# Expert gates scattered into HBM by accumulating indirect DMAs, and 42 in place of 32 sparse tokens, in a one-core decoder layer

## The chip, the core and the metric

The kernel runs on one NeuronCore of a Trainium2 chip. Its time is the device time of one execution in microseconds, lower is better. The engines are TensorE (PE, with PEld for its weight loads), VectorE (DVE), ScalarE (ACT), GpSimd (POOL) and SyncE (SP). SP and ACT issue direct DMAs; POOL issues the indirect ones, which take row numbers from on-chip memory. All DMAs run on the core's 16 DMA engines. The kernel's matmuls are done in single precision by splitting each operand into a high and a low part.

## The reference, cut to what matters

A decoder layer on 256 tokens of width 2048: a mixer, a cross attention and an expert layer. Only the last changes here. Each token scores 128 keys twice in each of 8 heads, keeps the 16 best of each list, then the 16 best of their 256 sums, and so picks 8 x 16 = 128 of 16384 experts, each with a gate.

```python
s1, i1 = lax.top_k(s[:, :, 0], 16)
s2, i2 = lax.top_k(s[:, :, 1], 16)
cand_s = s1[..., :, None] + s2[..., None, :]
top_s, top_pos = lax.top_k(cand_s, 16)       # per token and head, of 256
gates = softmax(top_s)                        # 8 heads x 16 = 128 a token
u = take(expert_u, experts)                   # rows of 2048
act = gelu(einsum('tkd,td->tk', u, x))
y = einsum('tk,tkd->td', gates * act, take(expert_v, experts))
```

## The kernel before

**Dense and sparse tokens.** The tokens are divided. The first TD = 224 are dense: all 16384 experts are computed for them, and the activations of experts not picked are multiplied by a gate of zero. The last TS = 32 are sparse: for them only the picked rows of the expert tables are fetched.

**Front.** 180 pieces of weights, each 128 x 1024 numbers of 4 bytes (512 KB), carry the mixer, the cross attention and the query projection. Each piece is loaded by SP into one of RAW = 4 buffers, copied to a high part by ACT (`whi`), and its low part (`wlo = raw - whi`) is made by POOL (`rest_of`, L438). PE then multiplies. A piece's buffer is loaded again when its low part is done; `whi` and `wlo` have SPL = 3 buffers, freed by PE.

**U stage.** 256 pieces hold the first expert table. Two pieces are a chunk of 128 experts (128 chunks). `u_piece` does per piece 8 wide matmuls (L1885: high weights, moving 448 columns, the tokens' high and low parts side by side) and 8 narrow ones (L1888: low weights, 224 columns). DVE joins the two halves of the sums (`join`, L1234), ACT applies GELU. PE uses three PSUM banks, so chunk c waits for what was done with chunk c-3. POOL makes all the low parts. Early in the stage PE does two sets of key products and DVE the top-k, written between its joins by hand; the tables are there at chunk C_TABLES = 48.

**Gates.** From chunk 54 on PE builds the gates: for each pair of dense tokens two one-hot matmuls of 256 columns (`gate_products`, L1899), 112 pairs. DVE makes the one-hot operands (L1376, L1382), joins the product (L1405) and multiplies it into the activations W (L1412).

**V stage.** 256 pieces of the second table (`v_piece`, L1982 wide and L1985 narrow), the same widths. ACT makes the high part; the low part is made by POOL for the first 8 pieces, then by DVE (`v_step`, L1437), which also splits the gated activations (L1439).

**Sparse rows.** In the V stage POOL gathers quarter rows by indirect DMAs (L465): partition = quarter x 32 + token, 128 x 512 numbers, 128 gathers for each table, into a ring of 12 buffers. DVE takes one after the other: a multiply with sum for table U (L1445), a multiply-add for V (L1458). The functions `taken_u` and `taken_v` say after which piece DVE takes each, and `issued_u`, `issued_v` in which order POOL asks for them; 128 rows in 105 pieces for U.

**Order.** Each engine's program is written out by hand; an engine executes its instructions in that order and waits on semaphores. A wait on DVE thus holds all low parts behind it, and those hold PE.

## Time and profile before

| what | value |
|---|---|
| median of 3 runs | 1914.01 us (1913.36 to 1915.1) |
| profiled execution, its span | 1912.2 us |
| PE busy | 1896.7 us, 11798 matmuls |
| DVE busy | 1383.4 us, 2585 instructions |
| POOL busy | 1390.8 us, 708 instructions |
| ACT busy | 950.5 us |
| DMA | 448.29 MB, mean 234 GB/s |

### The profile page before, as it was taken

Reading aid. Unit: us, or ns where it says so; the run is one execution under the profiler, and the core shown is the slowest. Engines: PE = TensorE matmul, PEld = TensorE weight load, DVE = VectorE, ACT = ScalarE, POOL = GpSimd, SP = SyncE. Lnnn points to the kernel's source line nnn. Section 1 sums busy time; section 2 is a strip of 40 time slices with the busy share of each in tenths; the row PEclk is TensorE's granted clock in tenths of the full one; section 3 lists DMA queues with packets and bytes.
Section 4 is the critical chain, followed back from the end, with each engine's and each line's share of the span. In section 5 each row is a group of like instructions: output and inputs, shape, how many; then the busy total and the mean of one; then the engine's idle time right before and its main releaser. Section 6 shows DMA issues by size and latency. Waiting matters only on the chain.

```text
span 1912.2 us, 35061 instructions
## 1 busy us (share of the span) xinstructions
PE 1896.7 (99%) x11798; PEld 1758.9 (92%) x11798; DVE 1383.4 (72%) x2585; ACT 950.5 (50%) x1342; POOL 1390.8 (73%) x708
## 2 busy tenths in 40 slices
PE   9999999999999999999999999999999999999997
PEld 7888889888999999999999999999999999999997
DVE  7534684045545777968888888479889889999986
...
DMA  8544546564655666666666566689999988999984
GB/s 307 186 143 153 199 144 224 193 190 155 218 188 177 207 209 208 210 202 196 194 192 196 189 195 195 200 280 351 333 336 334 333 297 298 337 325 334 328 273 145
DMA packets 128380, 448.29 MB, mean 234 GB/s; under 512 B 16528, under 2 KB 19472, under 8 KB 127632
## 3 DMA queue, kind: packets, MB, share of 16 engines
...
HBM read 443.04 MB, written 4.19 MB: 234 GB/s over the span
## 4 chain that ended last, share of the span: by engine, by line
PE 72%; POOL 17%; issue 8%; DMA 1%; DVE 1%; ACT 0%; POOLq 0%; SPq 0%; DVEq 0%; ACTq 0%
PE ps L1885 22%; PE ps L1982 22%; POOL wlo L438 17%; PE ps L1888 12%; PE ps L1985 11%; PE ps L1899 1%; PE ps L1585 1%; PE ps L1587 1%; PE ps L1586 1%; PE ps L1961 1%; DMA raw<-in_w_front 0%; PE ps L1869 0%; DMA big<-in_x_t 0%; PE ps L1963 0%; ACT whi L539 0%
## 5 line engine op out<-in xcount | busy, mean ns | idle before, releaser
L438 POOL TENSOR_TENSOR wlo<-raw,whi 128x1024 fp32r<-128x1024 f32 x436 | 1057.6, 2430 | 207.9 <-ACT whi L539 193.1
L539 ACT ACTIVATE whi<-raw 128x1024 fp32r<-128x1024 f32 x435 | 461.2, 1060 | 633.7 <-PE ps L1888 361.8
L1885 PE MATMUL ps<-x_parts,whi 128*128 128x448 f32 x2048 | 588.9, 369 | 0.0
L1982 PE MATMUL ps<-gate_parts,whi 128*128 128x448 f32 x1992 | 573.6, 369 | 0.0
L734 ACT ACTIVATE whi<-raw 128x1024 fp32r<-128x1024 f32 x256 | 271.7, 1061 | 294.9 <-PE ps L1985 255.8
L1888 PEld LDWEIGHTS ps<-x_parts,wlo 128*128 128x128 f32 x2048 | 384.7, 188 | 31.3
L1985 PEld LDWEIGHTS ps<-gate_parts,wlo 128*128 128x128 f32 x1992 | 374.2, 188 | 30.8
L1888 PE MATMUL ps<-x_parts,wlo 128*128 128x224 f32 x2048 | 386.9, 270 | 0.0
L1985 PE MATMUL ps<-gate_parts,wlo 128*128 128x224 f32 x1992 | 376.0, 270 | 0.0
L1437 DVE TENSOR_TENSOR wlo<-raw,whi 128x1024 fp32r<-128x1024 f32 x248 | 303.9, 1225 | 68.1 <-ACT whi L734 52.1
L1885 PEld LDWEIGHTS ps<-x_parts,whi 128*128 128x128 f32 x2048 | 310.3, 191 | 0.0
L1982 PEld LDWEIGHTS ps<-gate_parts,whi 128*128 128x128 f32 x1992 | 301.2, 191 | 0.1
L1585 PE MATMUL ps<-whi,x_parts 128*128 128x512 f32 (+1 forms) x544 | 214.1, 394 | 2.3 <-DVE wlo L888 2.3
L1587 PE MATMUL ps<-whi,x_parts 128*128 128x512 f32 (+1 forms) x544 | 210.1, 386 | 0.0
L1586 PE MATMUL ps<-wlo,x_parts 128*128 128x512 f32 (+1 forms) x544 | 209.4, 385 | 0.0
L465 POOL DMA_INDIRECT gather_low<-in_w_v,big x88 | 115.9, 1317 | 110.7 <-DVE big L1458 80.3
L465 POOL DMA_INDIRECT gather_low<-in_u_rows,big x88 | 103.9, 1180 | 67.3 <-DVE big L1445 54.3
L1234 DVE TENSOR_REDUCE big<-ps 128x224 f32<-128x448 f32 x128 | 79.4, 620 | 88.2 <-PE ps L1888 87.7
L1585 PEld LDWEIGHTS ps<-whi,x_parts 128*128 128x128 f32 x544 | 102.5, 188 | 23.8 <-DVE x_parts L868 3.5
L1587 PEld LDWEIGHTS ps<-whi,x_parts 128*128 128x128 f32 x544 | 102.6, 189 | 21.7
L1586 PEld LDWEIGHTS ps<-wlo,x_parts 128*128 128x128 f32 x544 | 102.7, 189 | 20.2
L1439 DVE TENSOR_TENSOR gate_parts<-big,gate_parts 128x224 fp32r<-128x224 f32 x256 | 112.7, 441 | 1.1 <-ACT gate_parts L737 0.6
...
## 6 DMA issues: line engine op xcount, KB each, us to landing
raw<-in_w_u SPq DMA_DIRECT2D x256, 512.0 KB
raw<-in_w_v SPq DMA_DIRECT2D x256, 512.0 KB
raw<-in_w_front SPq DMA_DIRECT2D x180, 512.0 KB
...
```

The source lines that it names most:

```text
L438: nc.gpsimd.tensor_tensor(wlo[:, j % SPL, :], raw[:, j % RAW, :], whi[:, j % SPL, :], ALU.subtract).then_inc(lo_done, 1)
L465: nc.gpsimd.indirect_dma_start(ROW[at_row], None, table, bass.IndirectOffsetOnAxis(index.bitcast(I32), 0)).then_inc(row_in[at_row], 16)
L539: nc.scalar.activation(whi[:, j % SPL, :], raw[:, j % RAW, :], ACT.Copy).then_inc(hi_done, 1)
L734: nc.scalar.activation(whi[:, (V0 + j) % SPL, :], raw[:, j % RAW, :], ACT.Copy).then_inc(hi_done, 1)
L1437: nc.vector.tensor_tensor(wlo[:, s, :], raw[:, j % RAW, :], whi[:, s, :], ALU.subtract).then_inc(lo_v_done, 1)
L1585: nc.tensor.matmul(out_ap, sh, mh, start=start, stop=False)
L1586: nc.tensor.matmul(out_ap, sh, ml, start=False, stop=False)
L1587: return nc.tensor.matmul(out_ap, sl, mh, start=False, stop=stop)
L1885: nc.tensor.matmul(sums[:, 0:2 * TD], whi[:, s, cols], x_parts[:, :, m, 0:TD], start=m == 0, stop=False, skip_group_check=True)
L1888: ins = nc.tensor.matmul(sums[:, TD:2 * TD], wlo[:, s, cols], xh[:, m, 0:TD], start=False, stop=m == DC - 1, skip_group_check=True)
L1982: nc.tensor.matmul(sums[:, 0:2 * TD], whi[:, s, cols], gate_parts[:, g, :, 0:TD], start=False, stop=False, skip_group_check=True)
L1985: ins = nc.tensor.matmul(sums[:, TD:2 * TD], wlo[:, s, cols], gate_parts[:, g, 0, 0:TD], start=False, stop=False, skip_group_check=True)
```

## The change

- The dense tokens become 214 and the sparse ones 42. PE's moving widths become 428 and 214. P // 3 = 42 tokens are three times on the partitions (GROUPS = 3, 126 rows), and each group handles 43 of a token's 128 experts (PER = 43). A gather now brings 128 whole rows of 2048 numbers (1.049 MB); there are 43 for each table, 86 in all, into a ring of 3. `taken` spreads them over pieces 18 to 121 and 128 to 234 of the V stage.
- The gate products on PE, their one-hot operands and joins on DVE are gone. A scratch tensor in HBM of 16384 experts x 224 numbers (14.7 MB) is filled with zeros in the front by 16 DMAs on ACT's queue. After the top-k, DVE computes the cell of each gate, and POOL adds the gates into the scratch by 256 indirect DMAs of single numbers, one for each of 128 slots and two blocks of tokens (128 and 96 partitions). Before the DMAs of a head it waits for those of the head before in the same block.
- Then POOL loads the gates back, 4 chunks at a time (32 loads, two buffers), and DVE multiplies them into W (`scale_by_gate`): 24 between the joins of chunks 112 to 126, 8 in the first pieces of the V stage.
- POOL's low parts in the U stage end with piece 71, and DVE takes one of twelve before that (`low_u`, piece 10 of a body). From piece 72 on DVE makes all low parts of the U stage, and all of the V stage.
- The top-k is written more densely (`topk_work`: a join after every 4200 ns of work as estimated in the code) and ends within 36 chunks. One of its lists of values now lies in PSUM, so that the sums of candidates have one operand in SBUF.
- At the end the three partial sums of the sparse tokens are moved to the same partitions by DMAs and added by DVE.

```diff
-C_TABLES, C_GATE = 48, 54
-C_ONES = C_GATE - 2
-TD, TS, PARTS, PD = 224, 32, 4, 512
-TOK_PAIRS = TD // 2
-RING = 12
+C_TABLES = 36
+E_BODIES = C_TABLES // CHUNKS_PER_BODY
+GROUPS = 3
+TS = P // GROUPS
+TD = T - TS
+PER = -(-P // GROUPS)
+PITCH = -(-TD // 16) * 16
+PER_LOAD = 4
+LOADS = NK // PER_LOAD
+SCALED_FROM, SCALED_IN_U = 112, 24
+RING = 3
...
-def issued_v(e):
-    return 117 + e if e < RING else taken_v(e - RING) + 1
-
-
-def taken_v(e):
-    return 132 + e * 21 // 25
...
+ROWS_FROM, WEIGHTS_AT_PIECE, ROWS_UNTIL = 18, 127, 234
+ADDED_AT = (*range(240, 239 + GROUPS), 251)
+
+
+def taken(n):
+    if n < PER:
+        return ROWS_FROM + n * (WEIGHTS_AT_PIECE - 6 - ROWS_FROM) // PER
+    return WEIGHTS_AT_PIECE + 1 + (n - PER) * (ROWS_UNTIL - WEIGHTS_AT_PIECE) // PER
...
+TOPK_NS = 4200
...
+        def low_of_u(i, j, late):
+
+            if late:
+                return lo_u_done, i * BODY + (j + 1 - E_BODIES * (BODY - 1))
+            if j == U_VECTOR:
+                return lo_u_done, i + 1
+            return lo_done, i * (BODY - 1) + (U0 + j + (j < U_VECTOR))
+
+        def low_of_v(i, j):
+
+            return lo_v_done, i * BODY + (j + 1)
...
+            with pool.Fori(U0 // BODY, U0 // BODY + E_BODIES) as i:
+                for j in range(BODY):
+                    if j != U_VECTOR:
+                        rest_of(i * BODY, j)
+
+            pool.wait_ge(zeros_out, 16 * NK // (2 * PER_LOAD))
+            pool.wait_ge(cells_ready, 1)
+            for head in range(PH):
+                for tb in range(TB):
+                    if head:
+                        pool.wait_ge(scattered[tb], 16 * TOPK * head)
+                    tokens = min(P, PITCH - tb * P)
+                    for k in range(TOPK * head, TOPK * (head + 1)):
+                        nc.gpsimd.indirect_dma_start(gates_d, bass.IndirectOffsetOnAxis(CELLS[0:tokens, tb, k:k + 1].bitcast(I32), 0),
+                                                     TOP_GATES[0:tokens, tb, k:k + 1], None,
+                                                     compute_op=ALU.add).then_inc(scattered[tb], 16)
+            for tb in range(TB):
+                pool.wait_ge(scattered[tb], 16 * TOPK * PH)
+
+            def load_gates(k):
+
+                if k >= 2:
+                    pool.wait_ge(scaled_by_gate, k - 1)
+                pool.dma_start(gates_of[:, k % 2].rearrange("p a b -> p (a b)"),
+                               gate_rows[:, k * PER_LOAD * PITCH:(k + 1) * PER_LOAD * PITCH]
+                               ).then_inc(gates_in[k % 2], 16)
+
+            def gather(n):
+
+                if n < RING:
+                    pool.wait_ge(used, V0)
                 else:
-                    pool.wait_ge(used, V0 + 4 + d)
-                gather(d % RING, u_rows, IDX[0][:, d:d + 1])
-
-            def gather_v(e):
-
-                if e < RING:
-                    pool.wait_ge(rows_taken, P - RING + (e + RING - P % RING) % RING + 1)
-                else:
-                    pool.wait_ge(rows_taken, P + e - RING + 1)
-                gather(e % RING, v_rows, IDX[1][:, e:e + 1])
-
-            asked = [0, 0]
-            for j in range(OPENING, 2 * NK):
-                if j == OPENING:
-                    pool.wait_ge(picks, 1)
-                    pool.wait_ge(used, V0)
-                while asked[0] < P and j >= issued_u(asked[0]):
-                    gather_u(asked[0])
-                    asked[0] += 1
-                while asked[1] < P and j >= issued_v(asked[1]):
-                    gather_v(asked[1])
-                    asked[1] += 1
-            assert asked == [P, P]
...
+            for k in range(SCALED_IN_U + 2):
+                load_gates(k)
+            pool.wait_ge(picks, 1)
+            for n in range(RING):
+                gather(n)
+            for k in range(SCALED_IN_U + 2, LOADS):
+                load_gates(k)
+            for n in range(RING, 2 * PER):
+                gather(n)
...
+            def zero_gates(q):
+                act.wait_ge(zeros_ready, 1)
+                some = 2 * PER_LOAD * PITCH
+                act.dma_start(gate_rows[:, q * some:(q + 1) * some],
+                              gates_of.rearrange("p a b c -> p (a b c)")).then_inc(zeros_out, 16)
...
+            def low_u(n0, n):
+                dve.wait_ge(hi_done, n0 + (U0 + n + 1))
+                nc.vector.tensor_tensor(wlo[:, (U0 + n) % SPL, :], raw[:, n % RAW, :], whi[:, (U0 + n) % SPL, :],
+                                        ALU.subtract).then_inc(lo_u_done, 1)
+
             def join(k0, c):
 
                 dve.wait_ge(used, k0 * 2 + (U0 + 2 * (c + 1)))
                 sums = ps[:, c % ACT_BANKS, 0:2 * TD].rearrange("p (h t) -> p t h", h=2)
-                late = not isinstance(k0, int) or k0 + c >= C_ONES
-                nc.vector.reduce_sum(LATE[:, c % ACT_BANKS, :] if late else W[:, k0 + c, :], sums, AX).then_inc(sums_joined, 1)
+                nc.vector.reduce_sum(W[:, k0 + c, :], sums, AX).then_inc(sums_joined, 1)
+                if not isinstance(k0, int) or C_TABLES - 2 <= k0 + c < NK - 2:
+                    low_u(k0 * 2, 2 * c + 4)
...
-            v = small(ROWS, 2, TOPK)
+            v = (small(ROWS, TOPK), ps[:, 3, 0:ROWS * TOPK].rearrange("p (r k) -> p r k", r=ROWS))
...
+            cells = CELLS.rearrange("p a b -> p (a b)")
+            step(nc.vector.scalar_tensor_tensor(cells, CH[:, 0, :], float(NK), CH[:, 1, :], ALU.mult, ALU.add))
+            dve.wait_ge(token_in, 16)
+            for tb in range(TB):
+                ins = nc.vector.tensor_scalar(CELLS[:, tb, :].bitcast(I32), CELLS[:, tb, :], float(PITCH),
+                                              stats[:, TOKEN + tb:TOKEN + tb + 1], ALU.mult, ALU.add)
+            ins.then_inc(cells_ready, 1)
...
+            def scale_by_gate(k):
+                dve.wait_ge(act_taken, PER_LOAD * (k + 1))
+                dve.wait_ge(gates_in[k % 2], 16 * (k // 2 + 1))
+                some = W[:, PER_LOAD * k:PER_LOAD * (k + 1), :]
+                nc.vector.tensor_tensor(some, some, gates_of[:, k % 2, :, 0:TD], ALU.mult).then_inc(scaled_by_gate, 1)
+
+            scaled = 0
+            for c in range(SCALED_FROM // CHUNKS_PER_BODY * CHUNKS_PER_BODY, NK - 1):
+                join(0, c)
+                while scaled < SCALED_IN_U * (c + 1 - SCALED_FROM) / (NK - 1 - SCALED_FROM):
+                    scale_by_gate(scaled)
+                    scaled += 1
+            assert scaled == SCALED_IN_U
...
-            def gate_products(i, j):
-
-                pe.wait_ge(hot1, i * PAIRS_PER_BODY + (j + 1))
-                pe.wait_ge(hot2, i * PAIRS_PER_BODY + (j + 1))
-                if not (isinstance(i, int) and i == 0 and j < 2):
-                    pe.wait_ge(gated, i * PAIRS_PER_BODY + (j - 1))
-                for m in range(2):
-                    ins = nc.tensor.matmul(ps[:, 4 + j % 2, m * 2 * P:(m + 1) * 2 * P], hot1_row[:, m, :],
-                                           hot2_rows[:, j % 2, m].rearrange("p a b -> p (a b)"), start=True, stop=True)
-                ins.then_inc(gate_mat, 1)
...
-            def u_row(slot):
-                dve.wait_ge(row_in[slot % RING], 16 * (slot // RING + 1))
...
+            def row_taken(n):
+                dve.wait_ge(row_in[n % RING], 16 * (n // RING + 1))
+                row, k = ROW[n % RING], n % PER
+                weight = WEIGHTS[:, k:k + 1]
+                if n < PER:
+                    ins = nc.vector.tensor_tensor_reduce(row, row, X_GAINED, 1.0, 0.0, ALU.mult, ALU.add, SUMS[:, k:k + 1])
+                elif k == 0:
+                    ins = nc.vector.tensor_scalar(X_GAINED, row, weight, None, ALU.mult)
+                else:
+                    dve.wait_ge(rows_taken, n)
+                    ins = nc.vector.scalar_tensor_tensor(X_GAINED, row, weight, X_GAINED, ALU.mult, ALU.add)
+                ins.then_inc(rows_taken, 1)
...
-                while done[0] < P and j >= taken_u(done[0]):
-                    u_row(done[0])
-                    done[0] += 1
...
+                while done < 2 * PER and j >= taken(done):
+                    row_taken(done)
+                    done += 1
```

POOL's program, at the end of its low parts, of the kernel before (gather_low and x_back hold the ring):

```order
L438 TENSOR_TENSOR wlo<-raw,whi 128x1024
L458 REGISTER_ALU
L458 COMPARE_AND_BRANCH
L465 DMA gather_low<-in_u_rows,big 128x512 x8
L465 DMA x_back<-in_u_rows,big 128x512 x4
```

and of the changed kernel at the same place:

```order
L475 TENSOR_TENSOR wlo<-raw,whi 128x1024
L499 REGISTER_ALU
L499 COMPARE_AND_BRANCH
L512 DMA gates_scratch<-big 3670016x1 x256
L522 DMA gates_of<-gates_scratch 128x896 x26
L532 DMA x_back<-in_u_rows,big 128x2048
L532 DMA gather_low<-in_u_rows,big 128x2048 x2
L522 DMA gates_of<-gates_scratch 128x896 x6
```

The 256 additions and 26 loads of gates now stand between the last low part and the first gather.

DVE's program in the V stage, while rows of table U are taken, of the kernel before (ISA is the multiply with sum and the reading of its sum):

```order
L1437 TENSOR_TENSOR wlo<-raw,whi 128x1024
L1439 TENSOR_TENSOR gate_parts<-big,gate_parts 128x224
L1445 ISA x_back,big<-x_back,big 128x512
L1445 ISA big 128x1
L1445 ISA gather_low,big<-gather_low,big 128x512
L1445 ISA big 128x1
L1437 TENSOR_TENSOR wlo<-raw,whi 128x1024
```

and of the changed kernel:

```order
L1458 TENSOR_TENSOR wlo<-raw,whi 128x1024
L1460 TENSOR_TENSOR gate_parts<-big,gate_parts 128x214
L1458 TENSOR_TENSOR wlo<-raw,whi 128x1024
L1460 TENSOR_TENSOR gate_parts<-big,gate_parts 128x214
L1468 ISA gather_low,big<-gather_low,big 128x2048
L1468 ISA big 128x1
L1458 TENSOR_TENSOR wlo<-raw,whi 128x1024
```

One or two quarter rows a piece became one whole row in two or three pieces.

DVE's program late in the U stage of the changed kernel (`gates_of` holds the loaded gates):

```order
L1303 TENSOR_REDUCE big<-ps 128x214
L1296 TENSOR_TENSOR wlo<-raw,whi 128x1024 x2
L1445 TENSOR_TENSOR big<-big,gates_of 128x856 x2
L1303 TENSOR_REDUCE big<-ps 128x214
L1296 TENSOR_TENSOR wlo<-raw,whi 128x1024 x2
L1445 TENSOR_TENSOR big<-big,gates_of 128x856
```

The multiplications by gates stand in DVE's queue behind a join and ahead of the next two low parts.

## Rows read from the trace of the kernel before

**Rows 1.** the page: busy time and parts 2 and 3, forty slices of 47.8 us

```profile
PE 1896.7 (99%) x11798; PEld 1758.9 (92%) x11798; DVE 1383.4 (72%) x2585; ACT 950.5 (50%) x1342; POOL 1390.8 (73%) x708
DMA  8544546564655666666666566689999988999984
```

**Rows 2.** the chain of waits, share of the span by engine

```profile
PE 72%; POOL 17%; issue 8%; DMA 1%; DVE 1%; ACT 0%; POOLq 0%; SPq 0%; DVEq 0%; ACTq 0%
```

**Rows 3.** waits of PE: who it waited for, us in total, times, longest

```profile
PE ps L1585 <- DVE wlo L888: 2.3, 1, 2.3
```

**Rows 4.** windows: us, busy us (x instructions) by engine, clock, DMA share, GB/s

```profile
660.00:720.00 60.00, 60.00 (x383) 57.07 (x382) 43.95 (x161) 28.33 (x37) 57.51 (x25) 1.00 0.66 209
1279.50:1289.50 10.00, 10.00 (x65) 9.53 (x64) 8.14 (x14) 5.52 (x9) 5.12 (x4) 1.00 1.02 396
1290.00:1300.00 10.00, 10.00 (x65) 9.53 (x64) 9.68 (x21) 5.28 (x9) 8.17 (x7) 1.00 0.99 358
1380.00:1440.00 60.00, 60.00 (x383) 57.07 (x382) 53.60 (x106) 32.15 (x48) 34.39 (x30) 1.00 0.95 337
```

**Rows 5.** line L1885: duration ns min/median/max, first and last start us

```profile
L1885 PE MATMUL ps<-x_parts,whi x2048: 362/367/452, 571.3 to 1250.8; 128*128 128x448 f32 x187
```

**Rows 6.** timeline of PE in the U stage: start us, us, what, count

```profile
700.46 0.38 PE L1888 MATMUL ps<-x_parts,wlo 128*128 128x224 f32 x2
700.67 0.57 PE L1885 MATMUL ps<-x_parts,whi 128*128 128x448 f32 x2
```

**Rows 7.** timeline of PEld there: two narrow loads, then two wide

```profile
700.26 0.39 PEld L1888 LDWEIGHTS ps<-x_parts,wlo 128*128 128x128 f32 x2
700.57 0.30 PEld L1885 LDWEIGHTS ps<-x_parts,whi 128*128 128x128 f32 x2
```

**Rows 8.** the gate matmuls L1899, and one pair of them in the timeline

```profile
L1899 PE MATMUL ps<-hot_rows,hot_row x224: 280/282/285, 854.7 to 1215.9; 128*128 128x256 f32 x112
903.53 0.40 PE L1899 MATMUL ps<-hot_rows,hot_row 128*128 128x256 f32 x2
903.77 0.56 PE L1885 MATMUL ps<-x_parts,whi 128*128 128x448 f32 x2
```

**Rows 9.** timeline of DVE in the V stage

```profile
1400.85 0.68 DVE L1445 CUSTOM_DVE_ANT_0 x_back<-x_back,big 128x512 f32<-128x512 f32 x1
1401.46 1.22 DVE L1437 TENSOR_TENSOR wlo<-raw,whi 128x1024 fp32r<-128x1024 f32 x1
1402.60 0.38 DVE L1439 TENSOR_TENSOR gate_parts<-big,gate_parts 128x224 fp32r<-128x224 f32 x1
1402.90 0.69 DVE L1445 CUSTOM_DVE_ANT_0 x_back<-x_back,big 128x512 f32<-128x512 f32 x1
1403.84 1.23 DVE L1437 TENSOR_TENSOR wlo<-raw,whi 128x1024 fp32r<-128x1024 f32 x1 [0.24 <-issue]
```

**Rows 10.** lines by form on DVE: busy us, mean ns of one

```profile
L1289 DVE TENSOR_TENSOR big<-big 128x256 f32<-128x256 f32 x16 | 26.5, 1696 | 0.0
L868 DVE SCALAR_TENSOR_TENSOR x_parts<-ps,big,x_parts 128x256 fp32r<-128x256 f32 x32 | 13.5, 478 | 31.6 <-ACT x_parts L560 31.6
```

**Rows 11.** timeline of POOL: gathers issued back to back

```profile
1271.42 0.96 POOL L465 DMA_INDIRECT gather_low<-in_u_rows,big  x1 [0.30 <-issue]
1272.69 0.95 POOL L465 DMA_INDIRECT gather_low<-in_u_rows,big  x1 [0.30 <-issue]
...
1401.20 1.15 POOL L465 DMA_INDIRECT gather_low<-in_u_rows,big  x1 [1.57 <-DVE big L1445]
1402.66 1.15 POOL L465 DMA_INDIRECT x_back<-in_u_rows,big  x1 [0.31 <-issue]
1404.11 1.77 POOL L465 DMA_INDIRECT x_back<-in_u_rows,big  x1 [0.30 <-issue]
1406.24 0.94 POOL L465 DMA_INDIRECT x_back<-in_u_rows,big  x1 [0.36 <-DVE big L1445]
```

**Rows 12.** DMA issues: KB each, us from issue to landing

```profile
big<-x_scratch ACTq DMA_DIRECT2D x4, 64.0 KB, 2.5
```

579 lines of the change are left out of this document (246 added, 333 removed).

## The prediction

> **What bounds the kernel now.** I read the page first. PE is busy 1896.7 of 1912.2 us [rows 1], and the chain of waits gives it 72% of the span [rows 2]. The 17% of POOL there say little: the waits of PE name one wait of 2.3 us at the start as the longest, and the others are smaller [rows 3]. So PE is fed on time, and what counts is the pace at which it starts matmuls. The windows give it: 383 matmuls in 60 us in the U stage and in the V stage alike, 16 a piece, which is 60/383 x 16 = 2.507 us a piece, at the full clock of 1.00, the level of 2.4 GHz [rows 4]. 512 pieces are 1284 us, two thirds of the span. The reader is to see also how near the others are. The DMA's line stands at 9 in most slices of the V stage [rows 1], its share is 0.95 at 337 GB/s there, against 0.66 at 209 in the U stage [rows 4], and DVE is busy 53.6 of 60 us. A change that takes work from PE in the V stage must find room there.
>
> **Gate products, removed.** A pair of gate matmuls stands between a narrow and a wide one: it starts at 903.53, and the next wide one at 903.77, so it costs 0.24 us [rows 8]. There are 112: 26.9 us of PE's own time, gone. DVE's work for them (one-hots, joins, products) goes too; PE never waited for it, so I cost that at nothing. What replaces it in the U stage is on DVE two low parts a chunk of 1.14 us (1401.46 to 1402.60) [rows 9] beside a join: under 3 us of the 4.9 of a chunk. ACT's work is no more than before.
>
> **Narrower matmuls.** Two narrow matmuls take 0.21 us from start to start (700.46 to 700.67) [rows 6], 0.105 each, and the four of a group 0.627, so a wide one 0.208. A column at 2.4 GHz is 0.417 ns. 448 to 428 columns gives 8.3 ns, 8 times a piece: 67 ns. For the narrow ones the bounds are 0 and 10 x 0.417 x 8 = 33 ns. Their 224 columns last 93 ns, less than the 105 of their step. The load records tell why: of two loads in 0.39 us with 0.19 each, the second begins at 700.46, the next load at 700.57 [rows 7], and its matmul at 700.67 [rows 6]. A load follows a load after 0.11 us and its matmul 0.10 later, so the load sets the step and fewer columns give nothing. I take 0: 67 ns a piece, 2.440 us, 34.3 us over 512. The Trainium skill (TensorE: Matmul & The Clock Gate, LDWEIGHTS) says that a load's time goes with its columns, 128 at 1.2 a ns, which is 107 ns. By that rule the sum is the same, and the trace agrees with 0.11 us; a rule of columns alone would make it 51.2.
>
> PE alone would then need 1912.2 - 26.9 - 34.3 = 1851.0 us.
>
> **Zeros and memset.** 16 stores of 0.92 MB go out among the front's loads. DMA stands at 4 to 6 tenths there after the first slice [rows 1] and four loads are in flight, which hides them; uncovered, 14.7 MB at 337 GB/s would be 44 us, but no slice of the front is full enough for more than a few us. I take 0, with 5 as upper end. The memset on POOL lies ahead of its first low part, which waits anyway.
>
> **Denser top-k.** DVE must keep PE's pace of 4.88 us a chunk with a join in each 4.2 us of work. The sum of candidates costs 1696 ns for 256 elements with both operands in SBUF while POOL works, where an instruction of 256 elements with one operand in PSUM takes 478 [rows 10]. 16 of them save 19 us. Work of 4.2 us, a join of 428 sums (0.30 for 224 elements, 1402.60 to 1402.90, and 1.05 ns for each more [rows 9], 0.51) and a sixth of a low part are 4.90, as much as PE takes. I take 0, upper end 10 us, since a low part of DVE is due one chunk after its join.
>
> **The additions, from POOL's last low part to the first use of a gate.** The U stage goes from 571.3 to 1250.8 [rows 5]. Of 679.9 us, 641.8 are its pieces and 26.9 the gates, which leaves 11 for the key products. In the changed kernel piece 71 starts at 571.3 + 11 + 71 x 2.44 = 755.5, and POOL is free some 2.4 us before: 753. DVE needs gate 0 when chunk 112 is joined: 571.3 + 11 + 226 x 2.44 = 1134. In these 381 us POOL issues 256 DMAs, the last must land and the first load too, twice 2.5 us by a small transfer [rows 12]. So an issue may take 376/256 = 1.47 us. The trace has no addition in HBM, only gathers of 128 rows. Back to back they start every 1.27 us (1271.42 to 1272.69) when DVE has little to do, and in the full V stage after 1.46, 1.45 and 2.13 us (1401.20 to 1406.24) [rows 11], 1.68 in the mean. The longest, of 1.77 us, began at 1404.11, within DVE's low part of 1403.84 [rows 9], which reads two operands from SBUF; POOL seems to wait for its end. In the V stage DVE does such work for 2.05 of 2.51 us, 82%, in the additions' stretch for 2.28 of 4.88, 47%. Between 1.27 and 1.68 that is 1.27 + 0.41 x 0.47/0.82 = 1.50. 256 x 0.03 = 8 us late, less a slack of some 2 on DVE: I take 6. Bounds: 0 (1.27) and 54 (1.68). Behind the waiting multiplication stand the joins and low parts, so PE stops for the whole of it. That an addition on 16 engines may itself be slower than the issue is left to the rival.
>
> **The V stage.** DVE: low part 1.14, gate part 0.30 [rows 9], 1.44 a piece. A row of 512 takes 0.61 (1400.85 to 1401.46), and 1024 elements 1.14 and 224 elements 0.30, so 2048 0.30 + 1824 x 1.05 ns = 2.2. One in 103/43 = 2.40 pieces: 0.92. Sum 2.36 of 2.44 us: DVE fits, with 3% left, where before 1.44 + 1.22 x 0.61 = 2.18 of 2.51 left 13%. DMA: 43 gathers of 1.049 MB in 103 pieces and 43 in 107, with 210 loads of 0.524 MB, are 90.2 + 110.1 = 200.3 MB in 210 x 2.44 = 512.4 us, or 391 GB/s. Before, the rate was 337. What the engines can do: when the ring filled the windows show 396 GB/s at a share of 1.02, then 358 at 0.99 [rows 4], 377 in the mean; 200.3/0.377 = 531.3, 19 us more than PE needs. Bounds: 396, 506 us, nothing lost; and 337/0.95 = 355, 564 us, 52 lost. I take 19: the mean of two windows at the limit. Of the DMA the Trainium skill (DMA: Bandwidth & Descriptors, Where 436 GB/s comes from) says that for HBM to SBUF the 358 of HBM bind. By that figure the 200.3 MB take 559.5 us and the loss is 47. The trace differs in a window of 10 us, where 396 came through, and comes to it in the next.
>
> **The end.** Adding three groups over whole rows puts some 9 us of DVE work into pieces 240 to 252, with about 1 us spare a piece and its tail's product of whole rows beside the last matmuls; stores are 4% smaller. I take 0, bounds -1 and 4.
>
> **Sum.** 1851.0 + 6 + 19 = 1876.0 for the profiled execution. The median of the runs lies 1.8 above its span, so 1878.
>
> **Rivals.** (A) Both covers hold: the additions are issued in under 1.47 us and the DMA carries 391 GB/s. For it: 396 in one window, and rows of 8 KB come in fewer descriptors than those of 2 KB. Against: the mean over any longer stretch. 1853. (B) The V stage is held by DMA and DVE together: with 3% left DVE can't catch up after a late row, and a late row holds the low parts. For it: the share of 0.95 now. Price: the 52 us of the bound in place of 19, and up to 5 more: 1911 to 1916, about the time of before. (C) Slower: the additions are issued, or carried out, too slowly. Place: the first multiplication by gates, at chunk 112. Each 0.1 us of the 256 costs 25.6 us. The gain left is 1914 - 1878 = 36, plus the 6 already counted, so from 1.47 + (42 + 4)/256 = 1.65 us it is slower. For it: 1.68 is the mean of the three issues quoted, 2.13 the longest, and an addition must read, add and write in HBM beside full loads. Against: DVE occupies its operand path half as much there, and half the DMAs have only 96 partitions. At 1.75 us: 72 late in place of 6, 1944. (D) The change doesn't lower the pace at all, widths of 214 starting at odd places: 34 lost, 1912.
>
> **How the numbers follow.** Forecast (one or both covers partly gone, 1858 to 1898): 0.50. A: 0.19. B: 0.12. C: 0.14. D: 0.05. The predicted time is the forecast's, 1878; its own range is 1858 to 1898. The range for 8 in 10 takes A and B in and ends inside C: 1848 to 1922. A measurement tells 0.2%, some 4 us, from no change. Faster by more: the forecast, A, half of B and a fifth of D, in all 0.76, and 0.02 of C: 0.78. Within: 0.06. Slower: 0.16.
>
> **What would show it.** Right: no L1899 rows; 60 us of U stage hold 393 to 394 matmuls (16 x 60/2.44); narrow matmuls still 0.21 us for two. In the V stage the DMA share is at 1.0, the rate above 365 GB/s, and PE waits for DVE low parts that waited for rows or for ACT's high parts behind a load. The additions take 1.4 to 1.6 us from start to start and DVE waits a few us for `gates_of` once. Wrong: narrow steps of 0.20 would give up to 17 us more; a wait of tens of us before L1445 is C; a V stage of 2.44 us a piece is A.

## The result, and the profile after

| | median of the runs | span of the profiled execution | clock of TensorE |
|---|---|---|---|
| before | 1914.55 us (1913.36 to 1915.56, 4 runs) | 1912.2 us | 0.997 |
| after | 2108.41 us (2108.12 to 2112.88, 4 runs) | 2106.9 us | 0.950 |

The changed kernel is slower: the ratio is 1.102, with a 95% interval of 1.100 to 1.103. The forecast was 1878 us in a range of 1848 to 1922.

The page after, its lines of busy time, clock and transfers and its chain of waits; they answer to [rows 1, 2]. A slice is 52.7 us.

```profile
PE 1864.5 (88%) x11578; PEld 1746.1 (83%) x11578; DVE 1362.0 (65%) x1914; ACT 947.8 (45%) x1342; POOL 1256.6 (60%) x629
...
PEclk9999999999999999999999555898999999999999
DMA  8656666658556577777776222799999998999985
GB/s 299 206 174 203 208 245 215 224 178 245 190 183 216 190 212 213 215 212 215 213 215 183 0 0 0 252 308 308 373 367 356 372 371 304 361 363 357 346 302 162
...
POOL 46%; issue 15%; DVE 15%; DMA 13%; PE 9%; ACT 2%; POOLq 0%; SPq 0%; DVEq 0%; ACTq 0%
```

PE is busy 1864.5 us (1896.7 before), 88% of the span in place of 99%. Three slices in the middle move 0 GB/s, and TensorE's clock there is at 0.5, the level of 1.2 GHz. The chain belongs to POOL now, where PE had 72%. The waits after (who waited, for whom, us in total, times, longest), which answer to [rows 3]:

```profile
DVE big L1445 <- DMA gates_of<-gates_scratch: 197.4, 16, 180.6
PEld ps L1903 <- DVE wlo L1296: 187.0, 6, 179.6
PE ps L1903 <- DVE wlo L1296: 186.6, 6, 179.4
ACT whi L787 <- DMA raw<-in_w_v: 183.2, 94, 7.5
POOL wlo L475 <- ACT whi L588: 170.3, 141, 23.9
ACT whi L787 <- PE ps L1972: 146.5, 126, 3.4
```

One wait of 179.4 us is nearly the whole difference of 194.7. L1445 is the multiplication by gates, L1296 a low part queued behind it on DVE. The windows (columns as in [rows 4]) show the U stage early, beside additions, in the stop and after it, and last the V stage:

```profile
660.00:720.00 60.00, 60.00 (x393) 58.53 (x392) 55.07 (x196) 27.37 (x34) 53.21 (x22) 1.00 0.64 211
1060.00:1120.00 60.00, 60.00 (x394) 58.59 (x393) 37.42 (x38) 29.43 (x37) 51.65 (x25) 1.00 0.79 213
1160.00:1220.00 60.00, 0.00 (x0) 0.00 (x0) 0.00 (x0) 0.00 (x0) 49.69 (x34) 0.50 0.21 0
1340.00:1400.00 60.00, 57.04 (x365) 54.76 (x364) 49.09 (x51) 27.75 (x34) 9.49 (x18) 1.00 0.93 330
1460.00:1720.00 260.00, 250.91 (x1600) 241.08 (x1600) 235.17 (x282) 130.84 (x198) 67.74 (x41) 1.00 0.94 363
```

393 and 394 matmuls in 60 us where before had 383: the pace forecast is there. (A window also counts the matmuls under way at its ends. From start to start an undisturbed piece takes 2.454 us, and before 2.520; the forecast had 2.440 and 2.507 from the counts. The difference, on which its sum rests, is the same.) In the third row nothing works but POOL. In the last, 1600 matmuls in 260 us are 2.60 us a piece, slower than before's 2.51 by the same count.

What POOL does then, first beside DVE's low parts with DVE's own timeline, then in the stop (start us, us, what, idle before):

```profile
899.22 2.15 POOL L512 DMA_INDIRECT gates_scratch<-big  x1 [0.31 <-issue]
901.67 2.15 POOL L512 DMA_INDIRECT gates_scratch<-big  x1 [0.30 <-issue]
904.12 2.21 POOL L512 DMA_INDIRECT gates_scratch<-big  x1 [0.30 <-issue]
...
898.84 1.23 DVE L1296 TENSOR_TENSOR wlo<-raw,whi 128x1024 fp32r<-128x1024 f32 x1 [0.37 <-ACT whi L588]
901.29 1.23 DVE L1296 TENSOR_TENSOR wlo<-raw,whi 128x1024 fp32r<-128x1024 f32 x1 [1.23 <-ACT whi L588]
903.81 1.23 DVE L1296 TENSOR_TENSOR wlo<-raw,whi 128x1024 fp32r<-128x1024 f32 x1 [0.43 <-ACT whi L588]
...
1250.04 1.43 POOL L512 DMA_INDIRECT gates_scratch<-big  x1 [0.30 <-issue]
1251.77 1.43 POOL L512 DMA_INDIRECT gates_scratch<-big  x1 [0.30 <-issue]
```

An addition starts 2.45 us behind the one before it, one for each low part of DVE, and 1.73 us with DVE idle. The forecast had 1.50. The additions' line in full (duration in ns, least, median, most; first and last start), and where the U stage began and ended, which answers to [rows 5]:

```profile
L512 POOL DMA_INDIRECT gates_scratch<-big x256: 1427/2087/2547, 759.3 to 1321.2; - x128
L1903 PE MATMUL ps<-x_parts,whi x2048: 352/370/726, 572.7 to 1402.4; 128*128 128x428 f32 x187
L1951 PE MATMUL ps<-gate_parts,whi x48: 367/373/697, 1407.9 to 2092.4; 128*128 128x428 f32 x48
```

They begin at 759, where 753 was forecast, and end at 1321, 187 us after the forecast had gate 0 due (1134). The U stage takes 829.7 us (before 679.5), the V stage 684.8 over all of its matmuls (before 647.6).

### The profile page after: what moved, and what is told of

Its sections match the earlier page's. It is cut to its first block, busy times and chain, and to the rows that moved or that the text cites. A ratio compares the mean times of both kernels' runs of the same rounds, so it can differ in the third digit from the quotient of the medians.

```text
span 2106.9 us, 32603 instructions
## 1 busy us (share of the span) xinstructions
PE 1864.5 (88%) x11578; PEld 1746.1 (83%) x11578; DVE 1362.0 (65%) x1914; ACT 947.8 (45%) x1342; POOL 1256.6 (60%) x629
## 4 chain that ended last, share of the span: by engine, by line
POOL 46%; issue 15%; DVE 15%; DMA 13%; PE 9%; ACT 2%; POOLq 0%; SPq 0%; DVEq 0%; ACTq 0%
POOL wlo L475 23%; POOL gates_scratch L512 23%; DMA raw<-in_w_v 11%; DVE wlo L1458 6%; PE ps L1969 4%; DVE big L1473 2%; PE ps L1972 2%; DVE gather_low L1468 2%; DMA gates_of<-gates_scratch 2%; ACT whi L787 2%; DVE gate_parts L1460 1%; DVE x_back L1468 1%; PE ps L1603 1%; PE ps L1605 1%; PE ps L1604 1%
## 5 line engine op out<-in xcount | busy, mean ns | idle before, releaser
L1903 PE MATMUL ps<-x_parts,whi 128*128 128x428 f32 x2048 | 582.6, 366 | 186.7 <-DVE wlo L1296 186.6
L475 POOL TENSOR_TENSOR wlo<-raw,whi 128x1024 fp32r<-128x1024 f32 x238 | 580.8, 2448 | 173.4 <-ACT whi L588 170.3
L1969 PE MATMUL ps<-gate_parts,whi 128*128 128x428 f32 x2000 | 572.9, 367 | 33.0 <-DVE gate_parts L1460 32.2
L512 POOL DMA_INDIRECT gates_scratch<-big x256 | 480.7, 1878 | 82.8 <-issue 82.8
L1906 PE MATMUL ps<-x_parts,wlo 128*128 128x214 f32 x2048 | 382.7, 268 | 0.0
L1972 PE MATMUL ps<-gate_parts,wlo 128*128 128x214 f32 x2000 | 375.4, 269 | 0.0
L1458 DVE TENSOR_TENSOR wlo<-raw,whi 128x1024 fp32r<-128x1024 f32 x256 | 313.0, 1223 | 80.6 <-ACT whi L787 80.3
L1296 DVE TENSOR_TENSOR wlo<-raw,whi 128x1024 fp32r<-128x1024 f32 x190 | 231.9, 1226 | 131.5 <-ACT whi L588 131.5
L1445 DVE TENSOR_TENSOR big<-big,gates_of 128x856 f32<-128x856 f32 x32 | 33.5, 1048 | 197.6 <-DMA gates_of<-gates_scratch 197.4
L532 POOL DMA_INDIRECT gather_low<-in_v_rows,big x29 | 61.7, 2128 | 148.6 <-DVE big L1473 108.0
L746 ACT ACTIVATE big<-big (+1 forms) x128 | 46.9, 367 | 198.5 <-DVE big L1303 198.5
```

The lines of the kernel that those rows point to most:

```text
L475: nc.gpsimd.tensor_tensor(wlo[:, j % SPL, :], raw[:, j % RAW, :], whi[:, j % SPL, :], ALU.subtract).then_inc(lo_done, 1)
L512: nc.gpsimd.indirect_dma_start(gates_d, bass.IndirectOffsetOnAxis(CELLS[0:tokens, tb, k:k + 1].bitcast(I32), 0), TOP_GATES[0:tokens, tb, k ...
L1296: nc.vector.tensor_tensor(wlo[:, (U0 + n) % SPL, :], raw[:, n % RAW, :], whi[:, (U0 + n) % SPL, :], ALU.subtract).then_inc(lo_u_done, 1)
L1458: nc.vector.tensor_tensor(wlo[:, s, :], raw[:, j % RAW, :], whi[:, s, :], ALU.subtract).then_inc(lo_v_done, 1)
L1903: nc.tensor.matmul(sums[:, 0:2 * TD], whi[:, s, cols], x_parts[:, :, m, 0:TD], start=m == 0, stop=False, skip_group_check=True)
L1906: ins = nc.tensor.matmul(sums[:, TD:2 * TD], wlo[:, s, cols], xh[:, m, 0:TD], start=False, stop=m == DC - 1, skip_group_check=True)
```

## The experiments

There are fourteen, all edits of the changed kernel; where one builds on another the text says so. Stage lengths are from the first to the last start of their matmuls. Those for which no range is given were run once, and differences under 5 us between them are not used.

**Half of the additions.**

```diff
-            for head in range(PH):
+            for head in range(PH // 2):
```

> Leaves out the gates of heads 4 to 7: 128 additions in place of 256, all else as in the changed kernel. Theory 1 (issue-bound additions): the 2.2 us a DMA on POOL is the whole cause of the 180 us stop before chunk 112; 128 x 2.44 = 312 us end at about 1072, ahead of chunk 112 at about 1134, so the stop is gone and the time is 2108 - 180 - 4 (clock at the lower level after the stop) = 1924, still slower than 1914 because the V stage keeps its loss of about 54 us. Theory 2 (the stop comes from the DMA engines, or the read-back of gates is slow by itself): a stop of tens of us stays, 1950 or more.

1924.8 us. The 128 additions stand 2.43 us apart and end at 1068, before they are due, and the stop is gone: the U stage takes 650.7 us. The V stage keeps its length, 680.7. The additions are the stop, and 10 us over the kernel before remain with them out of the way. This kernel is the base of most that follow.

**Writes in place of additions**, all 256.

```diff
-                                                     TOP_GATES[0:tokens, tb, k:k + 1], None,
-                                                     compute_op=ALU.add).then_inc(scattered[tb], 16)
+                                                     TOP_GATES[0:tokens, tb, k:k + 1], None).then_inc(scattered[tb], 16)
```

> The 256 indirect DMAs write the gates in place of adding them (where two heads of a token pick one expert, one gate is lost). Theory 1a (the addition makes the issue dear): the issue falls from 1.43 and 1.54 us to the 0.95 of a gather, spacing 1.25 with DVE idle, about 2.44 with DVE's low parts where it locks to them or less; time 2108 - 60 to 100. Theory 1b (it is the element-wise destination, not the addition): issue unchanged within 0.05 us, time within 5 us of 2108.

1935.9 us. The same numbers to the same cells, written, cost POOL 0.955 us each in place of 2.09:

```profile
L512 POOL DMA_INDIRECT gates_scratch<-big x256: 904/955/2013, 761.4 to 1099.5; - x128
```

They end at 1100 and there is no stop. A write costs what a gather cost ([rows 11], 0.95). So the price that I had carried over from a gather holds for a write, and not for an addition. The time is 70 us and more below what was expected, since the writes do not go at 2.44 us, one for each low part, but at 1.33 in the mean. The trace shows why:

```profile
903.39 0.95 POOL L512 DMA_INDIRECT gates_scratch<-big  x1 [0.30 <-issue]
...
908.44 1.94 POOL L512 DMA_INDIRECT gates_scratch<-big  x1 [0.30 <-issue]
...
903.41 1.23 DVE L1295 TENSOR_TENSOR wlo<-raw,whi 128x1024 fp32r<-128x1024 f32 x1 [1.23 <-ACT whi L587]
...
908.32 1.23 DVE L1295 TENSOR_TENSOR wlo<-raw,whi 128x1024 fp32r<-128x1024 f32 x1 [1.15 <-ACT whi L587]
```

The first write began just ahead of a low part (903.39, 903.41) and was not held, though the low part ran beside all of it. The second began 0.12 us inside one and ended 0.83 us behind its end. Of the 256 writes 21 were held in this way.

**Low parts with one operand in PSUM**, from piece 78 on; they subtract what lies there, and not the high part.

```diff
-                nc.vector.tensor_tensor(wlo[:, (U0 + n) % SPL, :], raw[:, n % RAW, :], whi[:, (U0 + n) % SPL, :],
+                other = ps[:, 4:6, :].rearrange("p a b -> p (a b)") if not isinstance(n0, int) or n0 + n >= C_TABLES * 2 + 6 else whi[:, (U0 + n) % SPL, :]
+                nc.vector.tensor_tensor(wlo[:, (U0 + n) % SPL, :], raw[:, n % RAW, :], other,
```

> DVE's low parts from piece 72 on of the U stage subtract two PSUM banks in place of the high part, so they read one operand from SBUF (their result is meaningless, their length and waits are the same). Theory 1 (POOL's issue waits for the end of DVE instructions with two SBUF operands): the spacing falls from 2.44 to the 1.73 and 1.85 us seen with DVE idle, the 256 end 256 x 0.65 x (161/256 of them were issued beside DVE) earlier, some 105 to 110 us; time about 2000. Rival (POOL is slowed by DMA traffic or by memory, not by DVE): spacing stays above 2.3 us and the time at 2108.

2016.4 us: 92 of the 194 us are back, where about 108 were expected. DVE's instruction takes 1.22 us as before, but POOL no longer waits for its end:

```profile
900.09 1.54 POOL L512 DMA_INDIRECT gates_scratch<-big  x1 [0.31 <-issue]
901.94 1.54 POOL L512 DMA_INDIRECT gates_scratch<-big  x1 [0.30 <-issue]
...
899.93 1.22 DVE L1297 TENSOR_TENSOR wlo<-raw,ps 128x1024 fp32r<-128x1024 f32 x1 [0.37 <-ACT whi L588]
902.38 1.22 DVE L1297 TENSOR_TENSOR wlo<-raw,ps 128x1024 fp32r<-128x1024 f32 x1 [1.23 <-ACT whi L588]
```

1.85 us apart beside DVE, as with DVE idle (1.84 in the mean over all 256). The stop is 86 us. The two causes are apart now: the addition itself (1.85 against 1.27 of a write) and DVE's instructions of two SBUF operands (2.45 against 1.85). They do not test the second. The writes above were held only where they began inside a low part and not where one began behind them, so what waits may be the reading at the start of an issue and not the descriptors.

**32 sparse tokens in place of 42.**

```diff
-GROUPS = 3
+GROUPS = 4
```

> Only the number of groups is set from 3 to 4: 32 sparse tokens, 224 dense, 64 whole rows in place of 86. Theory: the stop stays (POOL's issues are the same; PE reaches chunk 112 some 15 us later, so it is about 165 us) and the V stage loses no more than a few us, since its bytes fall from 391 to about 320 GB/s at PE's pace and DVE's rows from 0.92 to 0.67 us a piece. PE: 2.507 in place of 2.440 us a piece is +34. Sum 2108 - 15 + 34 - 54 = 2073. Rival (the V stage's loss has another cause than rows, as the loads of gates or the restart after the stop): 2120 to 2130.

2106.1 us (2104.1 to 2108.7, 3 rounds), ratio to before 1.100 (1.098 to 1.102), against 1.102 of the changed kernel. The stop is 177. The U stage is slower by PE's pace, 846.2, and the V stage faster, 667.4. Pieces 18 to 234 take 2.54 us each, 4 us over PE's own pace of 2.520 in all, where the changed kernel loses 38. So whole rows cost little as long as fewer of them come: the trace shows 331 GB/s from 1460 to 1720 in place of 363. What stays is the start of the V stage (13 us over PE's pace) and its last 22 pieces (5), and the stop is 12 us longer than the 165 reckoned; the time is 33 us above the 2073 expected. The ten tokens more bring PE what was forecast, and the transfers take it back.

**The first three gathers spread**, with half of the additions.

```diff
             for n in range(RING):
+                load_gates(SCALED_IN_U + 2 + 2 * n)
+                load_gates(SCALED_IN_U + 3 + 2 * n)
                 gather(n)
-            for k in range(SCALED_IN_U + 2, LOADS):
-                load_gates(k)
```

> Gates of heads 4 to 7 are left out, as in the run with half of the additions (1924.8 us, V stage 680.7), so that the stop in the U stage is absent. Here the first three gathers are issued between the last six loads of gates, about at pieces 6, 10 and 14 of the V stage, in place of all at once at its start. Theory: the slow start of the V stage (eight pieces at up to 4.5 us where 2.6 would do, with ACT waiting 6.8 and 7.0 us for a raw piece, and the clock that falls to 0.5 behind it) comes from the 3.1 MB of these gathers in front of the raw pieces; then the first eight pieces take at most 3 us each, the V stage 10 to 15 us less, the time is 1910 to 1915. Rival: the start is slow for the loads of gates and the multiplications that wait for them; then nothing moves by more than 3 us: 1922 to 1928.

1928.2 us, V stage 684.3: no gain, my theory falls. The first eight pieces take 3.6 us each (4.3 in the run with half of the additions), where at most 3 were expected, and pieces 18 to 234 take 7 us more in all. ACT still waits 7.4 us for a raw piece.

**Gathers of half width**, with half of the additions.

```diff
-                nc.gpsimd.indirect_dma_start(ROW[n % RING], None, u_rows if n < PER else v_rows,
+                w = D if n < RING else D // 2
+                table = u_rows if n < PER else v_rows
+                table = table if n < RING else table.rearrange("a (h b) -> (a h) b", h=2)
+                nc.gpsimd.indirect_dma_start(ROW[n % RING][:, (n // RING % 2) * (D - w):(n // RING % 2) * (D - w) + w], None, table,
```

> Gates of heads 4 to 7 are left out, and all gathers but the first three bring half of a row (0.52 MB in place of 1.05), while DVE works on the whole width as before; the sparse tokens' result is not computed. Compare with the run with half of the additions (1924.8 us, V stage 680.7, pieces 30 to 234 at about 2.62 us, where PE alone would need 2.44). Theory, the DMA engines bound the V stage (demand 391 GB/s): the pace goes to 2.45 us, the V stage loses 30 to 35 us, the time is about 1891. Rival, DVE bounds it (2.36 us of work a piece as forecast, more with its waits): the pace stays at 2.6, the time within 5 us of 1925. Half and half: 1905 to 1912.

1908.8 us, V stage 658.5, 22 us shorter: the case between the two rivals. Pieces 18 to 234 take 2.51 us each, where 2.45 was expected if transfers alone held them.

**Row work of half width on DVE**, its counterpart:

```diff
-                    ins = nc.vector.tensor_tensor_reduce(row, row, X_GAINED, 1.0, 0.0, ALU.mult, ALU.add, SUMS[:, k:k + 1])
+                    ins = nc.vector.tensor_tensor_reduce(row[:, 0:D // 2], row[:, 0:D // 2], X_GAINED[:, 0:D // 2], 1.0, 0.0, ALU.mult, ALU.add, SUMS[:, k:k + 1])
...
-                    ins = nc.vector.scalar_tensor_tensor(X_GAINED, row, weight, X_GAINED, ALU.mult, ALU.add)
+                    ins = nc.vector.scalar_tensor_tensor(X_GAINED[:, 0:D // 2], row[:, 0:D // 2], weight, X_GAINED[:, 0:D // 2], ALU.mult, ALU.add)
```

> Gates of heads 4 to 7 are left out, and DVE multiplies or adds only the first 1024 of a row's 2048 numbers; the gathers bring whole rows; the sparse tokens' result is not computed. The counterpart of the run with gathers of half width. Theory, DMA bounds the V stage: the pace stays near 2.6 us, time 1918 to 1927. Rival, DVE bounds it: DVE has 0.36 us less a piece (86 x 1.06 us / 256), the pace goes to 2.45, time about 1891.

1928.1 us, V stage 681.2: nothing. Pieces 18 to 234 take 565 us with half of the additions, 543 with narrow gathers and 567 with short row work. The window from 1300 to 1420 of the run with narrow gathers, and behind it that of the run with short row work:

```profile
1300.00:1420.00 120.00, 119.85 (x777) 116.52 (x776) 114.80 (x139) 64.63 (x97) 32.82 (x21) 1.00 0.86 300
```

```profile
1300.00:1420.00 120.00, 112.72 (x717) 108.11 (x716) 85.74 (x126) 58.23 (x89) 28.00 (x18) 1.00 0.94 358
```

With half the bytes DVE is busy 114.8 of 120 us, 96%, and PE hardly waits. With half of DVE's row work DVE is at 71%, and PE is still idle for 7 us of the 120 and has 717 matmuls, fewer than the other's 777. Of the two it is the transfers that hold the V stage there, and not DVE's row work.

**Writes, 32 tokens and spread gathers**, to see what the design could reach.

```diff
-GROUPS = 3
+GROUPS = 4
```

To this line come the edits of the writes and of the spread gathers, as shown above.

> Writes in place of additions (cells that two heads share keep one gate only), 32 sparse tokens (GROUPS = 4), and the first four gathers but one spread over pieces 6 to 14. It asks what the design could reach if the additions were cheap. From the parts: U stage 645 to 660 us at 2.51 us a piece plus the gap of 4.6 us at 722, V stage 667 less 6 to 12 for the spread gathers, 572.7 before them and 15 behind and between: 1900 to 1915 us, thus at most 0.7% faster than the kernel before, or the same. Rival: the width of 42 tokens is what pays, and this ends slower than the run with writes alone (1935.9).

2247.1 us, 1.173 times before. It missed by over 330 us, and in no part that I had thought of. From 785 to 1122 us PE does hardly anything:

```profile
850.00:950.00 100.00, 15.48 (x35) 10.36 (x36) 3.98 (x4) 3.73 (x5) 75.89 (x80) 0.50 0.05 11
```

The waits of PE over the whole run, most of them in that stretch, are put down to the instruction's issue and not to another engine:

```profile
PE ps L1905 <- issue: 139.9, 64, 3.2
PE ps L1902 <- issue: 138.1, 65, 3.9
```

**The same without the spread** (writes and 32 tokens alone):

> Writes in place of additions and 32 sparse tokens, the gathers at their old place: the run with writes, 32 tokens and spread gathers (2247 us) without its third edit. There PE stood at 70 instructions in 100 us from 785 to 1122 us, at half the clock, while POOL made its 256 writes; with writes and 42 tokens it did not. Theory: the spread has nothing to do with it, writes with 32 tokens do, by how PE's instructions are fetched beside them: again 2240 us. Rival: it hangs on the exact program, and this one runs free: 1920 to 1930.

1923.9 us. The same window:

```profile
850.00:950.00 100.00, 100.00 (x637) 95.17 (x637) 61.05 (x60) 47.85 (x60) 75.85 (x80) 1.00 0.69 207
```

The two programs differ only in POOL's list behind the writes and 26 loads of gates, at the start of the V stage (1242 us in this run). PE did 71 instructions in the 100 us while POOL did 80. Three runs of the stalled program took 2243 to 2248 us, the fourth 6166. It hangs on the exact program, and its cause stays open. It is not that more code was fetched: the page of either run has 40 packets of instructions, 0.66 MB, on queue q8. The run without it answers the question asked: with cheap issues (writes, which lose a gate where two heads pick one expert) the design ends 10 us behind the kernel before (1913.6 on that chip).

**Gains loaded early, gates multiplied from chunk 96**, on top of the spread gathers.

```diff
-SCALED_FROM, SCALED_IN_U = 112, 24
+SCALED_FROM, SCALED_IN_U = 96, 24
...
+            pool.wait_ge(picks, 1)
+            pool.dma_start(X_GAINED, gain_rows[0].partition_broadcast(P)).then_inc(gain_s_in, 16)
```

> Gates of heads 4 to 7 are left out. The first three gathers are spread as in the run before (1928.2 us, V stage 684.3); besides, the 1.05 MB row of gains is loaded in the U stage by POOL's queue in place of at piece 6 of the V stage, and the multiplications by gates begin at chunk 96 in place of 112. Theory: the DMA engines are full (share 1.01) from 1240 to 1255 in that run because rows of x, gains, gates, gathers and raw pieces fall together, and DVE waits 3.5 us for a load of gates at the turn of the stages. Then the gap at the turn (5.2 us) goes, the first eight pieces take under 3.2 us each (4.1 before), the time is 1912 to 1918. Rival: what slows the first pieces is the low clock that follows any gap; without the gap it gains the same in those pieces. Second rival: neither, it is the rows of x (three loads of 336 KB), which stay: 1922 to 1928.

1924.7 us, where the theory had 1912 to 1918. The gap at the turn of the stages is gone and the first eight pieces take 3.1 us each, as the theory had it. But the earlier multiplication met loads of gates that stood behind the gains, and PE waited 7.7 us before 1085; less this wait of my own making the time would be 1917. The second rival, the rows of x, is not out: the time lies in its range, and ACT still waits 6.5 us for a raw piece, at 1239.

**One load of x rows in place of three**, gains early, chunk 112 again.

```diff
-                    for g in range(GROUPS):
+                    for g in range(1):
```

> Gates of heads 4 to 7 are left out, and the rows of x are loaded for the first of three groups only (the others stay unfilled). First gathers spread, gains loaded in the U stage, the gate multiplications from chunk 112 as in the changed kernel. In the run with the latter two edits the packets of the three loads of x rows took 521 to 825 ns beside 310 of a gathered row of the same 8 KB, the DMA engines stood at 0.99 with 216 GB/s, and ACT waited 6.5 us for a raw piece. Theory: these loads make that wait; then it is under 2 us, no gap of PE over 1 us after the turn of the stages, the time 1914 to 1919. Rival: it comes from the gate loads and the sum of all: the wait stays over 4 us, the time 1920 to 1926.

1920.9 us, 2 above the range of the theory and inside that of its rival (1920 to 1926). The wait itself went as the theory had it: ACT's longest for a raw piece near the start is 2.3 us (from 6.5), the first eight pieces take 2.7 us each, and the V stage is 670.5, 8 us shorter than in the run before and 14 shorter than with the spread alone. So the loads of x rows make most of the slow start that was left once gains and gathers were out of their way.

Why they weigh so much is not shown. In the changed kernel they came in from 1416 to 1429, at a full share and a low rate:

```profile
1416.00:1430.00 14.00, 10.02 (x59) 9.30 (x57) 4.00 (x5) 1.78 (x4) 0.57 (x1) 0.85 1.02 258
```

Their 126 packets of 8 KB took 509 ns in the median. But gathered packets of 8 KB took 521 in the same stretch (309 from 1405 to 1700 over all), and the 4 KB packets of raw pieces 250 (159). All transfers were slow together. The Trainium skill (SBUF — State Buffer, Door 1: The DMA port swizzle) has a transfer's rate go by how many of 16 ports its partitions reach. That would be a reason for loads of 42 partitions to crowd the others, and no run here separates it from there being too many transfers at once; with four loads of 32 partitions (the run with 32 tokens) the packets of x rows took 521 ns too.

**The same, and gathers of half width:**

> The run with one load of x rows, and gathers of half width besides. Gates of heads 4 to 7 and the sparse tokens' result are left out. Theory, the V stage has lost its 56 us over PE's pace to two things, transfers at its start and the gathers' bytes: then it takes 635 to 645 us (256 pieces at 2.44 are 624.6) and the time is 1888 to 1898. Rival: a third cost is left, DVE's queue, of 15 us or more: V stage over 650, time over 1902.

1896.3 us, V stage 648.5: the time as expected, the stage 4 us over its range. Of the 57 us that the changed kernel's V stage has over PE's pace, 36 are gone with these edits.

**Additions of 16 gates each**, half of the additions.

```diff
-                    tokens = min(P, PITCH - tb * P)
+                    tokens = 16
```

> The 128 additions of heads 0 to 3 bring 16 gates each in place of 128 or 96 (gates of the other tokens and heads are left out). Compare with the run with half of the additions: 1.54 us for one of 128 with DVE idle, 1.43 for one of 96, 2.15 beside DVE's low parts, one in each of them. Theory: POOL needs 1.1 us whatever the number and 3.6 ns for each (from the 0.12 us between 128 and 96), and locks stand in between: an addition of 16 takes 1.1 to 1.2 us alone and the spacing beside DVE is 1.6 to 2.4. Rival: the time is the length of DVE's instruction, and the spacing stays 2.43. The whole time moves little, 1920 to 1928, since no addition is waited for here.

The rival holds: the durations stay at 2148 ns in the median and the spacing at 2.43, whatever the number.

```profile
L512 POOL DMA_INDIRECT gates_scratch<-big x128: 1274/2148/2280, 760.0 to 1069.1; - x128
```

Two of the 128 began outside a low part; they show the number, 1274 ns where 128 gates take 1534. The theory had 1.6 to 2.4 for the spacing. Smaller additions would not have helped.

The traces tell when the two engines go in step. An issue that begins inside a low part goes on when the low part ends. In the median an addition of 96 or 128 gates then ends 1.31 us behind it, one of 16 gates 1.15 and a write 0.83. With the 0.30 us between two issues the next one begins 1.6, 1.45 or 1.13 us behind the low part. The next low part begins 1.22 us behind it (2.45 less 1.23). Additions of any size here come too late and are held again; writes mostly come before it and are not.

**The first head written**, all gates there, the rest of the additions kept, gathers spread, gains early.

```diff
-                                                     compute_op=ALU.add).then_inc(scattered[tb], 16)
+                                                     compute_op=ALU.add if head else ALU.bypass).then_inc(scattered[tb], 16)
```

> All gates are there. The cells of the first head hold zeros before, so its 32 issues are writes; the other 224 stay additions. The first gathers are spread and the gains are loaded in the U stage. Theory, POOL's issues set the stop, at the prices measured (writes 1.33 us apart, additions 2.44 beside DVE, 1.8 with DVE idle): the writes end near 802, 143 additions fit until 1152, the 81 left take 146 us, and the stop falls from 180 to about 155; the start of the V stage gives 4 to 10 more: about 2076 us, 2070 to 2086. Rival: the stop is set by what comes behind the additions (the first loads of gates, the multiplications, the low clock), and it falls less than 10 us: 2092 to 2104.

2077.7 us (2076.3 to 2080.8), ratio to before 1.086 (1.084 to 1.087). The stop is 153.1 us where 155 was worked out. So the three prices are enough to size the stop. It is the fastest kernel here with all gates added, and still slower than before; none was found that beats both.

## Why the prediction was wrong

**The additions: the step that failed.** The prediction let an addition cost what a gather costs, 1.27 to 1.68 us, took 1.50, and got 6 us of lateness. What it left to the rival was that the 16 engines carry an addition out more slowly than POOL issues it; that did not happen, their share is 0.21 in the stop. Measured is an issue of 2.44 beside DVE and 1.73 to 1.85 alone, and PE stopped for 179.4 us.

Two errors lie in this. First, that POOL's part of an addition costs the same as of a gather: it takes 1.54 us in place of 0.955 (write). That half have only 96 partitions saves 0.11, not more. This error alone is the stop of 86 us of the run with one operand in PSUM. Second, that waiting for DVE could be scaled by DVE's busy share. Writes 1.27 apart are seldom caught by the low parts (21 of 256, 1.33 in the mean). Additions are caught nearly every time (125 of 128 began inside a low part in the run with half of them) and go in step with DVE; this is the other 94 us.

From 759.3 to 1321.2 the mean is 2.20 us an issue: (2.20 - 1.47) x 256 = 187 us late. The queue began 6 us later than reckoned and its end took 2 more (the first gates were there at 1328.4), and DVE itself came to gate 0 at 1147.9, 14 later than 1134: 181 us, and DVE waited 180.6.

**The rival C had it.** Its place is right (the first multiplication, chunk 112, low parts queued behind it), and its rule of 25.6 us for each 0.1 us; its price of 1.75 was too low and its chance of 0.14 too. [rows 11] showed an issue of 1.77 in which POOL waited for DVE, and no row at all showed an addition. With no row, the upper bound of 1.68 should not have been that of a gather in another stage.

**Removed gates, narrower matmuls: right.** No gate matmuls are left, and 393 matmuls in 60 us are the forecast of 393 to 394. Narrow ones give nothing, as said: the step of two is 0.21 us as before, and the 0.066 us that a piece is shorter (2.520 to 2.454) are what the wide ones alone were to give.

```profile
700.47 0.38 PE L1906 MATMUL ps<-x_parts,wlo 128*128 128x214 f32 x2
700.68 0.57 PE L1903 MATMUL ps<-x_parts,whi 128*128 128x428 f32 x2
```

So 61 us were won and spent. Rival D is out.

**Zeros and top-k: right in size.** The front ends at 572.7 (before 571.3). The sums of candidates take 412 ns (1696 in [rows 10]). PE waits once, 4.3 us at 722; forecast 0 to 10. Ahead of it lies a stretch of 12 us between two joins (707.7 and 719.6). A copy of 2.62 us and two short instructions of 2.48 stand there, 7.6 us for which the code reckons 2.0. The two work on 256 numbers and take as long as one of POOL's low parts, which run back to back beside them (six in 14.93 us); that DVE waits for POOL there is likely and was not tested.

```profile
L1370 DVE TENSOR_TENSOR big<-big,ps 128x256 f32<-128x256 f32 x16 | 5.9, 412 | 0.0
...
711.66 2.48 DVE L1399 TENSOR_SCALAR big<-big 128x256 uint32<-128x256 uint32 x1
714.07 2.48 DVE L1400 TENSOR_SCALAR big<-big 128x256 uint32<-128x256 uint32 x1
...
726.60 0.73 PE L1903 MATMUL ps<-x_parts,whi 128*128 128x428 f32 x1 [4.29 <-DVE wlo L1296]
```

**The V stage: the mechanism right, the size low.** PE's pace of 2.454 x 256 is 628 us; the stage takes 684.8, 57 more (before 3 more than its own pace). The forecast was 19, bounds 0 and 52. It splits in three. Pieces 18 to 234: 38 us, against the 19. The rate that the transfers held is 363 GB/s at a share of 0.94 (the window above), not 377; 200.3 MB at 363 are 552 us, 37 over the 515 of 210 pieces. The mean of two windows of 10 us at the ring's filling was too high for a rate to hold over 500. With half of the additions the same pieces lose 35; half the bytes of the gathers take 22 of them away, half of DVE's row work nothing. 13 to 16 remain with the narrow gathers, at a share of 0.86, and are not explained. The start, pieces 0 to 18: 15 us, not forecast at all. Whole rows mean loads of x rows, gains and gathers of four times the size at the moment when nothing may be late, and the clock falls behind the gap:

```profile
1421.72 1.06 ACT L787 ACTIVATE whi<-raw 128x1024 fp32r<-128x1024 f32 x1 [5.27 <-DMA raw<-in_w_v]
1430.58 1.06 ACT L787 ACTIVATE whi<-raw 128x1024 fp32r<-128x1024 f32 x1 [7.53 <-DMA raw<-in_w_v]
...
1430.00:1440.00 10.00, 6.76 (x25) 6.48 (x26) 5.21 (x7) 3.99 (x6) 0.54 (x1) 0.52 1.01 404
```

The last 22 pieces: 4 us (none before).

**The turn of the stages**: 5 us, not forecast. DVE's last multiplication in the U stage waits for its load, which POOL issues when a buffer comes free; the first gate part of the V stage is queued behind it.

```profile
1405.28 1.05 DVE L1445 TENSOR_TENSOR big<-big,gates_of 128x856 f32<-128x856 f32 x1 [3.11 <-DMA gates_of<-gates_scratch]
1407.86 0.70 PE L1951 MATMUL ps<-gate_parts,whi 128*128 128x428 f32 x1 [4.94 <-DVE gate_parts L1460]
```

**The sum again**, with what was measured: PE alone 1851.0, the stop 179.4, the gap in the top-k 4.3, the turn 5, the V stage 57 less the 3 that 1851.0 holds already, 54. That is 2093.7 of 2106.9. Of the 13 left 4 are in the last chunks of the U stage (365 matmuls in 60 us in place of 393, beside loads of gates, at a DMA share of 0.93). A piece at the clock of 1.2 GHz behind the stop costs 2, and a slow one behind the gap in the top-k 1.5. The front is 1.4 longer, the matmuls that spread the tables at piece 71 take 1 more, the end behind the last matmul 1. Some 2 are left over.
